# Attention scores on one Trainium2 core: the keys' low part meets the queries' high part alone, in 64 rows of the array

## The reference, cut to what matters

```python
def one_block(qblk):                       # 128 queries, 8 heads, 2 key heads, head size 64
    s = jnp.einsum('bqkgd,bmkd->bkgqm', qblk, k).astype(jnp.float32) * scale
    p = jax.nn.softmax(s, axis=-1).astype(v.dtype)
    return jnp.einsum('bkgqm,bmkd->bqkgd', p, v)
```

## Time and profile before

| | |
|---|---|
| median of 3 executions | 1091.03 us (1091.01 to 1094.38) |
| the profiled execution | 1092.47 us, of which the span of its instructions is 1090.6 us |
| mean granted TensorE clock | 0.973 of full speed |
| TensorE busy | 989.9 us, 91% of the span |
| VectorE, ScalarE, GpSimd busy | 673.1, 585.0, 255.1 us |
| chain of work that ended last, by engine | TensorE 64%, DMA 13%, VectorE 9%, ScalarE 7% |
| attention units, first layer | from about 160 to 268 us of the span |
| attention units, second layer | from about 691 to 799 us of the span |

### The profile page before, as it was taken

The page is one execution under the profiler, slowest core; times in us unless marked ns, Lnnn a source line. Parts: engine busy times, 40 slices in busy tenths (PEclk is TensorE's granted clock), DMA queues, the critical chain, the costliest instruction groups (busy, mean ns, idle before and its releaser), DMA issues.

```text
span 1090.6 us, 16042 instructions
## 1 busy us (share of the span) xinstructions
PE 989.9 (91%) x5720; PEld 764.2 (70%) x5720; DVE 673.1 (62%) x966; ACT 585.0 (54%) x929; POOL 255.1 (23%) x304
## 2 busy tenths in 40 slices
PE   5999989996997899999889999899789969999984
PEld 2688865764875688777747888566668758888761
DVE  0359125655266799989552950565635779998946
ACT  4452235655232588877356322565633348888822
POOL 3033015211041222320320410520212322122131
PEclk9999999999899899999999999999989989999998
DMA  9785227543165899998581240556423269999944
GB/s 316 265 266 207 78 63 261 214 161 128 42 222 223 345 392 405 400 401 338 217 237 69 78 154 10 192 209 226 134 97 135 96 226 367 402 417 416 358 172 166
DMA packets 89091, 248.17 MB, mean 228 GB/s; under 512 B 25772, under 2 KB 30380, under 8 KB 79816
## 3 DMA queue, kind: packets, MB, share of 16 engines
q1 hardware_dynamic: 75960, 209.54, 51.9%
q0 software_dynamic: 11632, 32.60, 8.5%
q10 hardware_dynamic: 1440, 5.24, 1.2%
HBM read 220.82 MB, written 30.21 MB: 230 GB/s over the span
## 4 chain that ended last, share of the span: by engine, by line
PE 64%; DMA 13%; DVE 9%; ACT 7%; issue 4%; SPq 1%; POOL 0%; ACTq 0%; POOLq 0%; DVEq 0%
PE ps L1573 12%; PE ps L1575 11%; PE ps L1574 11%; DMA pool<-in_moe_w 9%; PE ps L1591 4%; PE ps L1769 3%; PE ps L1784 3%; PE ps L1580 3%; PE ps L1582 3%; PE ps L1581 3%; DVE wL L1360 2%; ACT wH L948 2%; PE ps L1758 2%; PE ps L1989 2%; PE ps L1759 2%
## 5 line engine op out<-in xcount | busy, mean ns | idle before, releaser
L1573 PE MATMUL ps<-wH,actH 128*128 128x512 f32 x608 | 247.1, 406 | 11.2 <-DVE actL L1493 7.4
L1575 PE MATMUL ps<-wH,actL 128*128 128x512 f32 x608 | 239.6, 394 | 0.0
L1574 PE MATMUL ps<-wL,actH 128*128 128x512 f32 x608 | 239.3, 394 | 0.0
L1360 DVE TENSOR_TENSOR wL<-raw,wH 128x2048 fp32r<-128x2048 f32 x64 | 146.3, 2286 | 13.4 <-ACT wH L948 13.1
L1573 PEld LDWEIGHTS ps<-wH,actH 128*128 128x128 f32 x608 | 115.7, 190 | 40.3 <-issue 11.9
L948 ACT ACTIVATE wH<-raw 128x2048 fp32r<-128x2048 f32 x64 | 122.3, 1913 | 27.5 <-DMA raw<-in_moe_w 27.5
L1575 PEld LDWEIGHTS ps<-wH,actL 128*128 128x128 f32 x608 | 115.5, 190 | 25.6
L1574 PEld LDWEIGHTS ps<-wL,actH 128*128 128x128 f32 x608 | 115.8, 190 | 21.9
L1580 PE MATMUL ps<-wH,actH 128*128 128x512 f32 x256 | 103.8, 405 | 6.0 <-DVE actL L1481 3.4
L1582 PE MATMUL ps<-wH,actL 128*128 128x512 f32 x256 | 100.8, 394 | 0.0
L1581 PE MATMUL ps<-wL,actH 128*128 128x512 f32 x256 | 99.9, 390 | 0.0
(11 more groups left out here) (264 smaller groups left out, 1698.3 us busy)
## 6 DMA issues: line engine op xcount, KB each, us to landing
raw<-in_moe_w SPq DMA_DIRECT2D x96, 512.0 KB, 8.2
raw<-in_w_ada SPq DMA_DIRECT2D x40, 1024.0 KB, 5.0
raw<-in_moe_w SPq DMA_DIRECT2D x16, 1024.0 KB, 13.9
pool<-in_moe_w SPq DMA_DIRECT2D x32, 512.0 KB, 8.1
pool<-in_moe_w SPq DMA_DIRECT2D x16, 1024.0 KB, 13.4
ys<-pool SPq DMA_DIRECT2D x32, 512.0 KB, 13.1
raw<-in_w_in SPq DMA_DIRECT2D x15, 1024.0 KB, 10.0
raw<-in_w_ada SPq DMA_DIRECT2D x16, 512.0 KB, 12.0
```

The lines of the kernel that those rows point to most:

```text
L1360: dve.tensor_tensor(wL[:, w, :], mraw[parity][i], f32(wH[:, w, :]), ALU.subtract).then_inc(sem(f"m_lo{i}"), 1)
L1573: pe.matmul(out, aH, wH[:, slot_, cols_], start=first, stop=False)
L1574: pe.matmul(out, aH, wL[:, slot_, cols_], start=False, stop=False)
L1575: return pe.matmul(out, aL, wH[:, slot_, cols_], start=False, stop=last)
```

## The change

For the latent tiles the scores are cut into two halves of 320 keys, one for each bank, in place of 512 and 128. The high part of the keys is still multiplied in 128 rows. The product with the low part takes the queries' high part alone, so it needs 64 rows: the first half of the keys uses rows 0 to 63, the second half rows 64 to 127. For the latter, the queries' high part must also lie in partitions 64 to 127; `q_out` writes it there with a further copy (`qH`). The maximum and the exponential read two pieces of 320 in place of one of 640. The context tile is computed as before.

```diff
+KEYS2 = 320
+        qH = actL[:, 3072:5120].rearrange("p (b h n) -> p b h n", b=2, h=NH)
...
                 def q_out(t, r):
                     act.wait_ge(sem("qT_psum"), at("qT_psum", l, 2 * t + r + 1))
+                    if t:
+                        act.activation(qH[HD:P, t % 2, 4 * r:4 * r + 4, :].rearrange("p h n -> p (h n)"), ps[0:HD, 7, :], ACT.Copy)
                     act.activation(qT[:, t % 2, 4 * r:4 * r + 4, :].rearrange("p h n -> p (h n)"), ps[:, 7, :], ACT.Copy
                                    ).then_inc(sem("qT"), 1)
...
-                        act.activation(prob[:, u % 2, 0:keys], flat[:, 2 * N * (u % 2):2 * N * (u % 2) + keys], ACT.Exp, bias=nmax[:, u % 2:u % 2 + 1],
+                        b0 = 2 * (u % 2)
+                        dst, src = ((prob[:, u % 2, :].rearrange("p (b n) -> p b n", b=2), ps[:, b0:b0 + 2, 0:KEYS2]) if t
+                                    else (prob[:, u % 2, 0:P], ps[:, b0, 0:P]))
+                        act.activation(dst, src, ACT.Exp, bias=nmax[:, u % 2:u % 2 + 1],
...
-                        dve.tensor_reduce(nmax[:, u % 2:u % 2 + 1], flat[:, 2 * N * (u % 2):2 * N * (u % 2) + keys], X, ALU.max, negate=True).then_inc(sem("nmax"), 1)
+                        src = ps[:, b0:b0 + 2, 0:KEYS2] if t else ps[:, b0, 0:P]
+                        dve.tensor_reduce(nmax[:, u % 2:u % 2 + 1], src, mybir.AxisListType.XY if t else X, ALU.max, negate=True).then_inc(sem("nmax"), 1)
...
-                        spans = [(0, 0, 512), (1, 512, 640)] if t else [(0, 640, 768)]
-                        for bk, a, b in spans:
-                            pe.matmul(ps[:, b0 + bk, 0:b - a], qT[:, t % 2, h, :], kk[:, 2 * v, a:b], start=True, stop=False)
-                            m = pe.matmul(ps[:, b0 + bk, 0:b - a], qT[:, t % 2, h, :], kk[:, 2 * v + 1, a:b], start=False, stop=True)
+                        if t:
+                            for bk in range(2):
+                                pe.matmul(ps[:, b0 + bk, 0:KEYS2], qT[:, t % 2, h, :], kk[:, 2 * v, bk * KEYS2:(bk + 1) * KEYS2], start=True, stop=False)
+                            pe.matmul(ps[:, b0, 0:KEYS2], qT[0:HD, t % 2, h, :], kk[0:HD, 2 * v + 1, 0:KEYS2], start=False, stop=True)
+                            m = pe.matmul(ps[:, b0 + 1, 0:KEYS2], qH[HD:P, t % 2, h, :], kk[HD:P, 2 * v + 1, KEYS2:2 * KEYS2], start=False, stop=True)
...
```

More of the change, by code:

```diff
@@ L1755, in _ @@
                         b0 = 2 * (u % 2)
-                        spans = [(0, 0, 512), (1, 512, 640)] if t else [(0, 640, 768)]
-                        for bk, a, b in spans:
-                            pe.matmul(ps[:, b0 + bk, 0:b - a], qT[:, t % 2, h, :], kk[:, 2 * v, a:b], start=True, stop=False)
-                            m = pe.matmul(ps[:, b0 + bk, 0:b - a], qT[:, t % 2, h, :], kk[:, 2 * v + 1, a:b], start=False, stop=True)
+                        if t:
[3 more added lines that the diff above has]
+                            m = pe.matmul(ps[:, b0 + 1, 0:KEYS2], qH[HD:P, t % 2, h, :], kk[HD:P, 2 * v + 1, KEYS2:2 * KEYS2], start=False, stop=True)
+                        else:
+                            pe.matmul(ps[:, b0, 0:P], qT[:, 0, h, :], kk[:, 2 * v, 640:768], start=True, stop=False)
+                            m = pe.matmul(ps[:, b0, 0:P], qT[:, 0, h, :], kk[:, 2 * v + 1, 640:768], start=False, stop=True)
                         m.then_inc(sem("scores"), 1)
```

## The result

| | before | changed |
|---|---|---|
| median of 4 executions | 1091.47 us | 1106.64 us (1105.27 to 1107.69) |
| ratio, with its 95% interval | 1 | 1.0125 [1.0102, 1.0148] |
| span of the profiled execution | 1090.6 us | 1104.1 us |

The change makes the kernel slower by 1.25%, 13.6 us by the ratio (11.1 to 16.1 by its interval) and 13.5 us by the spans; the two medians lie 15.2 us apart. The prediction was 10.4 us. Units are numbered as `u` in the code, from 0; the prediction's "units 9 to 32" are u = 8 to 31.

A forecast was written before the change was run, and what follows sets the result against it. TensorE was taken to bound the kernel (busy 91% of the span). Scores 3.6 + copies 1.6 = 5.2 us a layer, 10.4 us for both, giving a median of 1101.4 us; range 1092.5 to 1108.5.

The forecast's parts named there:

- the scores: Latent units' score matmuls on TensorE: net +0.18 us a unit, 20 units paying, 3.6 us a layer.
- changes of the array's part: Latent units' scores on TensorE: going from 128 rows to 64 and back costs 0.32 us a unit.
- the overlap: Latent units' scores: the two 64-row matmuls run at once, so 320 columns less save 0.14 us a unit.
- the copies: Further ScalarE copies that TensorE waits for at the latent tiles: 0.94 + 0.47 + 0.20 = 1.6 us a layer.
- rival without overlap: Scores: the 64-row halves don't run at once and nothing is saved; +15.6 us, 1106.6 us; chance 0.18.
- Units that hide it: Units 8, 9, 16 and 24 of the bound stretch: TensorE waits there anyway, so the slower scores cost nothing.
- no change charged: Scores: row halves entered and left without a drain; -1.2 us in all, 1089.8 us, read as no change; chance 0.12.
- cheap changes: Scores: two changes of rows cost 0.14 us, the unit comes out even; +3.9 us, 1095.0 us; chance 0.14.
- new wait: Bound stretch: TensorE newly waiting for the maximum or the exponential would prove the prediction wrong; no size given.

The follow-up runs named there:

- one-half kernel: Changed kernel without the further copies, with both low products in rows 0 to 63 so they can't run at once; ratio 1.0117.
- pieces: Kernel before with only the keys cut 320 + 320 in two banks, all score matmuls in 128 rows, no further copies; ratio 0.9965.
- halves alone: Changed kernel without the further copies, the second half of the keys taking the queries' low part in place of the high; ratio 1.0057.
- low first: Changed kernel with each unit's two 64-row matmuls ahead of the two in 128 rows; ratio 1.0099.
- alternate: Changed kernel with the score matmuls in the order 128, 64, 128, 64 rows; ratio 1.0387.
- copies alone: Kernel before with only ScalarE's further copies added, their output read by nothing; ratio 1.0067.

## Why the prediction was right, and where its sizes were off

**Direction and mechanism: right.** The prediction said slower by 10.4 us, 7.2 of it from the scores (changes of the array's part less the overlap) and 3.2 from the copies; measured were 13.6, inside the range and in the forecast's direction. Its two steps were each found alone in an experiment, and add to the whole.

**In part luck.** The median of 1106.64 us lies above the forecast's own range (1098 to 1105), on the time of the rival without overlap (1106.6); only the units' lengths and the halves' common start tell the two apart. And the sizes erred against each other: the scores were forecast at 3.6 us a layer and measured at 2.6, the copies at 1.6 and about 3.0; 0.3 lies under both. That gives 5.3 us a layer, almost the forecast 5.2, without either term being right. What stands above it went with the clock, which the sum left out.

**The scores: +0.18 forecast, +0.13 measured.** The two terms in it were right: two changes of the part 0.34 us (forecast 0.32; by the one-half kernel against the pieces), the halves' overlap 0.14 (forecast 0.14). The missing term is the cut, which goes the other way. I priced 1280 columns by the 0.227 us of 512 columns, as if a column cost the same everywhere. The two matmuls of 128 columns and the transposes behind them cost more, and the change removed them too: -0.07 us. 0.34 - 0.14 - 0.07 = 0.13. Over the 20 units that pay it is 2.6 us a layer (halves alone).

By the Trainium skill, page "TensorEngine Tiling (Array Packing)", section "Key Properties", a change of the tiling mode drains the engine. The runs agree that each change costs, also for rows alone: 0.16 us in low first, 0.17 by one half, 0.19 in alternate (0.34 - 0.15), and the weight loads stand idle for 0.19 us ahead of the 64-row matmuls. Whether that time is a drain, or a weight load that no longer runs under the matmul ahead, no run separates. By the Trainium skill, page "TensorE: Matmul & The Clock Gate", section "Part 3: Packing small matmuls — row/col tiling", matmuls in different row groups start about 4 ns apart; the trace's halves start in the same 0.01 us, which agrees.

**Units that hide it: right.** Units 16 and 24, behind the wait for the copy of probabilities, keep their length, and so do the last tile's units 32 to 37 together. Units 8 and 9 hide it too: with the halves alone they are as long together as before (1.85 and 2.39 us against 1.82 and 2.41).

**The copies: 1.6 us a layer forecast, about 3.0 measured.** I took 0.47 us for each from a pair of 128-row copies. The pair of a 64-row and a 128-row copy is 0.60 us apart, and the further copy starts 0.11 later behind another instruction. At units 17 and 25 the forecast had 0.18 + 0.10 = 0.28 us; measured are 0.47, and the copies alone give the same, so the slower scores of that unit lie under the wait. At unit 9 the forecast had 0.47; the copies alone give 0.73. In the first tile, where it had 0.94 for two copies, units 1 and 2 of the first layer grow by 0.73 and 0.60 us. The tile as a whole grows by 0.94, but that this is the forecast number is luck: unit 3 gave 0.40 back, because its eight records of `ada_mm` ran at a granted clock of 0.52 before and 0.67 after:

```profile
167.19 1.92 PE L1591 MATMUL ps<-raw,cpad 128*32 128x512 f32 x8
```

```profile
168.33 1.52 PE L1601 MATMUL ps<-raw,cpad 128*32 128x512 f32 x8
```

**Not in the sum: the clock.** Scores and copies make 4.0 us in units 8 to 31 (second layer) and 1.3 in the first tile (units 1 and 2 of the first layer), 5.3 us a layer, 10.6 of the 13.5. The rest goes with the clock. Unit 10 took 4.10 us in the first layer against 2.87 in the second, in the stretch whose clock was 0.63; it stands behind the 1.45 us wait at 179.28, but the like wait in the second layer (1.47 us at 718.30) was followed by no fall. In the second layer's first tile units 1 to 3 cost 2.4 us in place of 0.94, at a clock of 0.61 from 700 to 708. At the end of the first layer's last tile unit 38 took 4.97 us against 2.62 before, at 0.50 of the clock; in the second layer it was the other way round, 2.76 against 4.23. That these falls come from the copies isn't shown: the halves alone, with no further wait, lost 1.0 and 2.4 us in the first tile in the same way, and one half gained 1.3 in one layer.

**Rivals.** No overlap (0.18) and no change charged (0.12) are both excluded in this loop; cheap changes too. The new wait that I named as a way of being wrong did not appear.

## What to carry to other kernels

Count how often the array changes its part, not only the columns that a part saves: here two changes (0.34 us) cost more than the 320 columns that they saved (0.14 us), and the order of the work around them decides as much as the work. Even where the array changes its part anyway, so that one change is added and not two, the halves stay behind the even cut (2.48 us against 2.44). By these numbers (0.34 us for two changes, 0.44 ns a column) my estimate is that they pay from some 770 saved columns on; no run here has that many. When a change has several parts, run each alone: the one that was only a means, the even cut, is the only one that made the kernel faster, and alone it beats the kernel before and the changed one (0.9965, or 0.9961 as 384 + 256).

## What was not expected of the hardware

- Two matmuls of 128 columns behind two of 512 cost 0.07 us a unit more than the same columns in four matmuls of 256 to 384 or 320.
- A ScalarE copy of 512 columns in 64 partitions lasts as long as one in 128 (0.59 and 0.60 us), and the next copy starts 0.60 us behind it, not 0.47 to 0.50 as behind one in 128 partitions. It also starts 0.02 us behind the end of the instruction ahead, where the copy in 128 partitions started 0.09 ahead of that end. Why is open: this copy differs in its number of partitions and in that it moves from partitions 0 to 63 to 64 to 127.
- The clock's falls move between executions of nearly equal kernels: the first tile's eight units changed by -1.4 to +2.5 us in traces where nothing in them was changed.
